# Depthwise convolution of the mixers: two channel blocks on TensorE from four-tap stacks in four column tiles, one block on VectorE

## The reference, cut to what matters

```python
def conv_module(val, gate, w_dw, b_dw, ln_g, ln_b, w_pw, b_pw):
    h = val * jax.nn.sigmoid(gate)                       # (1, 256, 384)
    h = lax.conv_general_dilated(                        # causal, 31 taps, one filter per channel
        h, w_dw[:, None, :], window_strides=(1,),
        padding=((CONV_WIDTH_2 - 1, 0),),
        dimension_numbers=('NWC', 'WIO', 'NWC'),
        feature_group_count=D_CONV) + b_dw
    h = jax.nn.silu(layer_norm(h, ln_g, ln_b))
    return h @ w_pw + b_pw
```

## Time and profile before

| | |
|---|---|
| median of three runs | 1805.52 us (1805.26 to 1806.93) |
| the profiled execution: its own time | 1807.05 us |
| its span, first to last instruction | 1805.3 us |
| granted TensorE clock, mean | 0.996 |
| TensorE busy | 1738.2 us (96%) |
| VectorE busy | 1184.4 us (66%) |
| ScalarE busy | 915.0 us (51%) |
| GpSimd busy | 55.9 us (3%), 54.4 of it the diagonals |
| the 62 records a layer of L1027 (31 products, two passes each) | 13.42 us in layer 1 |

### The profile page before, as it was taken

How to read it: one execution, slowest core, us unless ns; L and a number is a source line. 1 busy time by engine, 2 the same in 40 slices (tenths; PEclk the granted TensorE clock), 3 DMA queues, 4 the chain that set the end, 5 groups by cost and what they waited for, 6 DMA issues and landing times.

```text
span 1805.3 us, 25215 instructions
## 1 busy us (share of the span) xinstructions
PE 1738.2 (96%) x10391; PEld 1425.7 (79%) x10391; DVE 1184.4 (66%) x1517; ACT 915.0 (51%) x992; POOL 55.9 (3%) x71
## 2 busy tenths in 40 slices
PE   7999998999999999999999999999999999999997
PEld 7988897899998999998777777776776777676774
DVE  6664576766798665579677665665665665765653
ACT  5445655555564444345565553554455554554542
POOL 0000000000060000050000000000000000000000
PEclk9999999999999999999999999999999999999999
DMA  9423443565544365645669999999999999999996
GB/s 325 153 94 124 150 146 102 178 233 196 164 157 142 133 220 184 203 126 208 233 210 344 374 398 385 398 396 396 398 391 378 396 396 398 398 398 398 397 397 252
DMA packets 243562, 495.14 MB, mean 274 GB/s; under 512 B 9609, under 2 KB 99439, under 8 KB 229103
## 3 DMA queue, kind: packets, MB, share of 16 engines
q1 hardware_dynamic: 238927, 489.04, 74.0%
q10 hardware_dynamic: 4512, 4.40, 0.9%
HBM read 492.36 MB, written 1.05 MB: 273 GB/s over the span
## 4 chain that ended last, share of the span: by engine, by line
PE 81%; DVE 10%; ACT 6%; issue 2%; DMA 0%; ACTq 0%; DVEq 0%
PE bank L567 22%; PE bank L569 21%; PE bank L568 21%; DVE splitL L2159 6%; PE bank L1233 4%; PE bank L1266 4%; ACT splitH L1461 4%; PE bank L1212 1%; DVE co L2615 1%; PE bank L1168 1%; PE bank L1027 1%; PE bank L596 1%; PE bank L710 1%; PE bank L733 0%; PE bank L1085 0%
## 5 line engine op out<-in xcount | busy, mean ns | idle before, releaser
L2159 DVE TENSOR_TENSOR splitL<-raw,splitH 128x2048 fp32r<-128x2048 f32 (+1 forms) x248 | 561.8, 2273 | 155.3 <-ACT splitH L1461 154.5
L1461 ACT ACTIVATE splitH<-raw 128x2048 fp32r<-128x2048 f32 (+2 forms) x250 | 469.5, 1889 | 123.2 <-PE bank L569 102.4
L567 PE MATMUL bank<-RAH,splitH 128*128 128x256 f32 x1088 | 312.5, 287 | 6.0 <-DVE RAL L2169 3.3
L568 PE MATMUL bank<-RAL,splitH 128*128 128x256 f32 x1088 | 308.5, 284 | 0.0
L569 PE MATMUL bank<-RAH,splitL 128*128 128x256 f32 x1088 | 308.5, 284 | 0.0
L567 PE MATMUL bank<-splitH,RBH 128*128 128x512 f32 x736 | 293.5, 399 | 3.3 <-DVE splitL L2159 3.3
L569 PE MATMUL bank<-splitH,RBL 128*128 128x512 f32 x736 | 287.4, 391 | 0.0
L568 PE MATMUL bank<-splitL,RBH 128*128 128x512 f32 x736 | 286.9, 390 | 0.0
L2159 DVE TENSOR_TENSOR splitL<-rawx,splitH 128x2048 fp32r<-128x2048 f32 x89 | 203.2, 2290 | 28.7 <-ACT splitH L1461 28.2
L567 PEld LDWEIGHTS bank<-RAH,splitH 128*128 128x128 f32 x1088 | 209.3, 192 | 10.4 <-DVE RAL L2169 4.5
L568 PEld LDWEIGHTS bank<-RAL,splitH 128*128 128x128 f32 x1088 | 209.4, 192 | 1.0
(11 more groups left out here) (340 smaller groups left out, 2223.6 us busy)
## 6 DMA issues: line engine op xcount, KB each, us to landing
raw<-in_moe_wg SPq DMA_DIRECT2D x71, 1024.0 KB, 10.4
raw<-in_moe_wd SPq DMA_DIRECT2D x69, 1024.0 KB, 11.5
raw<-in_moe_wu SPq DMA_DIRECT2D x68, 1024.0 KB, 11.2
rawx<-in_moe_wu SPq DMA_DIRECT2D x44, 1024.0 KB, 11.6
rawx<-in_moe_wd SPq DMA_DIRECT2D x43, 1024.0 KB, 12.4
rawx<-in_moe_wg SPq DMA_DIRECT2D x41, 1024.0 KB, 11.8
raw<-in_w_in SPq DMA_DIRECT2D x24, 1024.0 KB, 6.2
raw<-in_w_up SPq DMA_DIRECT2D x22, 1024.0 KB, 5.1
```

What stands on the lines that cost most here:

```text
L567: e.matmul(o, lh, rh, start=start, stop=False)
L568: e.matmul(o, lh, rl, start=False, stop=False)
L1461: return e.activation(o, src, ACT.Copy)
L2159: e.tensor_tensor(l[:, 0:size], raws[home[n]][:, 0:size], h[:, 0:size].bitcast(F), ALU.subtract)\
```

## The change

TensorE takes two blocks, 2 and 0 (in that order, v = 0 and 1), and VectorE keeps block 1. A product now sums over 4 taps x 32 channels on its 128 partitions and yields 32 channels. Four such products with i = 0 to 3 go to partitions 32i to 32i+31 of one bank, each in its own column tile; 8 groups g of four taps make the (padded) 32 taps, so a block has 8 x 4 = 32 products of 32 weight columns and 256 moving columns, and a layer has 64.

The moving data `hs[v]` hold for each i four copies of 32 channels of `hc`, copy j shifted by j columns. ScalarE makes them by DMA from SBUF to SBUF, 16 DMAs a block, 32 a layer. The weights `stack` come ready from DRAM, one DMA of 1 MB a layer, issued by ScalarE. GpSimd's diagonals go.

```diff
@@ tensor, mixers(l) @@
-                b = bank["dw", l] = ring.take()
-                t.wait_ge(S.dwdiag, 32 * l + 31)
-                t.wait_ge(S.th, 3 * l + 3)
-                o = claim(b, (S.co0, l + 1))
-                for k in range(31):
-                    mm = e.matmul(o[:, 0:256], diag[:, k, :], hc[:, 0, 2 + k:258 + k], start=(k == 0), stop=(k == 30))
-                mm.then_inc(S.dw, 1)
+                t.wait_ge(S.in_layer, 96 * (l + 1))
+                for v in range(2):
+                    b = bank["dw", l, v] = ring.take()
+                    t.wait_ge(S.hs, 512 * l + 256 * v + 256)
+                    o = claim(b, (S.co0, 2 * l + v + 1))
+                    for g in range(8):
+                        for i in range(4):
+                            mm = e.matmul(o[32 * i:32 * i + 32, 0:256], stack[:, v, i, g, :],
+                                          hs[v][:, i, 2 + 4 * g:258 + 4 * g], start=(g == 0), stop=(g == 7))
+                    mm.then_inc(S.dw, 1)
@@ scalar, mixers(l) @@
+                def shifted(v, u):
+                    a.wait_ge(S.th, 3 * l + v + 2)
+                    a.wait_ge(S.zero, 4)
+                    if v:
+                        a.wait_ge(S.hs, 512 * l + 256)
+                    for i in range(4):
+                        for j in range(4):
+                            load(hs[v][32 * j:32 * j + 32, i, :], hc[32 * i:32 * i + 32, u, j:j + 288], S.hs)
+
+                load(stack[:, :, :, :, :].rearrange("p v i g c -> p (v i g c)"), stacks[l], S.in_layer)
                 hi_to(mc[0] + 1)
 ...
                 take(mc[2])
+                shifted(0, 2)
                 gate_of(2, 0)
                 for _ in v_rows(mv, 384, lambda tb: vn[:, tb, :], S.mrow, slot, root):
                     pass
+                shifted(1, 0)
                 a.wait_ge(S.mrow, 6 * l + 2)
 ...
-                a.wait_ge(S.dw, l + 1)
-                e.activation(co[:, 0, :], banks[bank["dw", l]][:, 0:256], ACT.Identity,
-                             bias=pcol("conv_dw_b_2", 3 * l)).then_inc(S.co0, 1)
+                for v in range(2):
+                    a.wait_ge(S.dw, 2 * l + v + 1)
+                    e.activation(co[:, 2 - 2 * v, :], banks[bank["dw", l, v]][:, 0:256], ACT.Identity,
+                                 bias=pcol("conv_dw_b_2", 3 * l + 2 - 2 * v)).then_inc(S.co0, 1)
@@ vector, mixers(l): taps() now runs over k = 0 to 30 of block 1 alone @@
@@ gpsimd @@
+            e.memset(hc[:, :, 288:292], 0.0).then_inc(S.zero, 1)
             for l in range(2):
-                dwc = PCOL["conv_dw_w_2"] + 93 * l
-                g.wait_ge(S.xadd, 12 + 8 * l)
-                for k in range(31):
-                    e.tensor_scalar(diag[:, k, :], ident, prm[:, dwc + 3 * k:dwc + 3 * k + 1], None, ALU.mult)\
-                        .then_inc(S.dwdiag, 1)
```

More of the change, by code:

```diff
@@ L149, in halves, with program @@
     return (0, 2, 1, 3).index(tb_half) + 1
-def program(nc, x, mem, consts, w, out, cap):
+def program(nc, x, mem, consts, stacks, w, out, cap):
     ctx = ExitStack()
@@ L175, in program @@
         BL = [at(f"BL{i}", [128, 768], b0 + 64 * KB + 3 * KB * i) for i in range(2)]
-        diag = at("diag", [128, 31, 128], b0 + 64 * KB)
+        stack = at("stack", [128, 2, 4, 8, 32], b0 + 64 * KB)
+        hs = [at("hs2", [128, 4, 288], b0 + 72 * KB)]
         b0 += 40 * KB
@@ L1056, in mixers @@
                         b = bank["colsum", l] = ring.take()
-                        t.wait_ge(S.taps, 62 * (l + 1))
-                        t.wait_ge(S.co0, l + 1)
+                        t.wait_ge(S.taps, 31 * (l + 1))
+                        t.wait_ge(S.co0, 2 * l + 2)
                         o = claim(b, (S.dd, 6 * l + 3))
@@ L2598, in mixers @@
                 dwc = PCOL["conv_dw_w_2"] + 93 * l
-                tapped = [62 * l]
+                tapped = [31 * l]
                 def taps():
-                    at = {}
-                    order = [(k, 1) for k in range(3)]
-                    order += [(k - 3 * (u == 2), u) for k in range(3, 34) for u in (1, 2)]
-                    for k, u in order:
-                        if k < 31:
-                            o, src = co[:, u, :], hc[:, u, 2 + k:258 + k]
-                            wk = prm[:, dwc + u + 3 * k:dwc + u + 3 * k + 1]
-                            if k == 0:
-                                v.wait_ge(S.th, 3 * l + u)
-                                ins = e.tensor_scalar(o, src, wk, pcol("conv_dw_b_2", 3 * l + u), ALU.mult, ALU.add)
-                            else:
-                                v.wait_ge(S.taps, at[u])
-                                ins = e.scalar_tensor_tensor(o, src, wk, o, ALU.mult, ALU.add)
-                            ins.then_inc(S.taps, 1)
-                            tapped[0] += 1
-                            at[u] = tapped[0]
-                            yield
+                    o = co[:, 1, :]
+                    for k in range(31):
+                        src = hc[:, 1, 2 + k:258 + k]
+                        wk = prm[:, dwc + 1 + 3 * k:dwc + 1 + 3 * k + 1]
+                        if k == 0:
+                            v.wait_ge(S.th, 3 * l + 1)
+                            ins = e.tensor_scalar(o, src, wk, pcol("conv_dw_b_2", 3 * l + 1), ALU.mult, ALU.add)
+                        else:
+                            v.wait_ge(S.taps, tapped[0])
+                            ins = e.scalar_tensor_tensor(o, src, wk, o, ALU.mult, ALU.add)
+                        ins.then_inc(S.taps, 1)
+                        tapped[0] += 1
+                        yield
                 more = taps()
@@ L3245, with tap_stacks @@
            "ffn_wu_2", "ffn_wd_2", "moe_router_2", "moe_wg_2", "moe_wu_2", "moe_wd_2", "final_g_2"]
+def tap_stacks(taps):
+    rows = np.zeros((2, 32, 384), np.float32)
+    rows[:, 0:31] = taps
+    rows = rows.reshape(2, 8, 4, 3, 4, 32).transpose(0, 2, 5, 3, 4, 1)[:, :, :, [2, 0]]
+    stacks = np.zeros((2, 4, 32, 2, 4, 8, 32), np.float32)
+    for c in range(32):
+        stacks[:, :, c, :, :, :, c] = rows[:, :, c]
+    return stacks.reshape(2, 128, 2048)
 def kernel(**inputs):
@@ L3259 @@
     out = nc.dram_tensor("out_0", (1, 256, 1024), F, kind="ExternalOutput").ap()
-    program(nc, aps["x"], aps["mem"], aps["shape_constants"], {n: aps[n] for n in WEIGHTS}, out, CAP)
+    program(nc, aps["x"], aps["mem"], aps["shape_constants"], aps["stacks"], {n: aps[n] for n in WEIGHTS}, out, CAP)
     r = run_bass_kernel_spmd(nc, [feeds], core_ids=[0])
```

32 lines of the change are left out of this document (17 added, 15 removed).

## The result

The changed kernel takes 1816.49 us (median of five runs, 1812.85 to 1818.42), beside 1806.93 us for the kernel before in five runs (1805.26 to 1807.50). The ratio is 1.0054, with a 95% interval of 1.0043 to 1.0066. The forecast was 1799.2 us with a range to 1804.5. Among the rivals it is the slow DMA issues, which had 8% and gave 1811 us.

The account below looks back on a forecast made before the run. TensorE was taken to bound the kernel (81% of the chain); gains of 3.8 us in layer 0 and 3.9 in layer 1, less 1.4 for the clock, make 6.3 us: 1799.2 us from the median 1805.52, range 1793.5 to 1804.5.

Parts of the forecast that it names:

- the slow DMA issues: Rival, 8%: each issue holds ScalarE; slower than before from 0.51 us an issue, 1811 us at 0.6 us.
- TensorE's saving: Convolution on TensorE: four column tiles side by side take 7.1 instead of 13.5 us, 6.4 us saved in each layer.
- VectorE's saving: 31 taps fewer on VectorE, 12.3 us a layer, of which 0.48 us count in layer 0 and none in layer 1.
- ScalarE's issues: 16 DMAs issued in one go, twice a layer, on ScalarE: 0.37 us each, 5.9 us a group.
- The first group "fits": 16 issues ahead of the third sigmoid: 5.9 us fit in ScalarE's idle 6.52 and 6.51 us, costing nothing.
- The second group: 16 issues behind `vn`: `at_rows` late by 2.8 and 2.5 us in layers 0 and 1, lost by TensorE in full.
- The data of `hs`: Both groups issued by about 540 us, convolution begins at about 551, so a latency of several us is hidden.
- The clock: Longer TensorE waits ahead of the pooling may lower its granted clock: 1.4 us lost for both layers together.
- The stack's issue: Ahead of the second group of `RAH` on ScalarE: 0.3 us lost in layer 0, nothing in layer 1.
- The experts: TensorE sets the pace there, so time saved ahead stays saved; rival that they swallow it, 6%, 1805.5 us.
- tiles one after another: Rival, 4%: column tiles don't run side by side, the convolution takes 27.6 us a layer; 1837 us.
- the cheap issues: Rival, 4%: ScalarE's issues take 0.2 us or less, nothing is late; 13.3 us gained, 1792.3 us.

Follow-up runs that it names:

- the filled wait: The changed kernel with 15 products of constants (6.5 us) added on TensorE ahead of its wait for `at_rows`; 1813.85 us, ratio 1.0035.

## Why the prediction was wrong, step by step

- **TensorE's saving: right.** 7.1 us forecast, 7.05 measured in both layers, 6.46 us saved. The four tiles run at 0.98 of the ideal (32 x 0.216 = 6.9); the row of two tiles had given 0.96. The 8.7 us, estimated from the Trainium skill (TensorE: Matmul & The Clock Gate, "Part 3: Packing small matmuls"), didn't come.
- **VectorE's saving: right.** 0.48 us in layer 0, none in layer 1. But 31 x 0.397 was too much for what it is relieved of: see the last section.
- **ScalarE's issues: the step that failed.** "At 0.37 a group takes 5.9 us." An issue took 0.641 us and a group 10.3. I had sized it by ten small loads from DRAM on SyncE, and these DMAs have their source in SBUF. No row of the trace before showed such an issue; it was a case for a bound from further off. That trace had longer ones on ScalarE itself, from DRAM: the shortest for `pool_w` (32 KB) took 0.61 us, and the rows of 1.5 us were set aside as queued behind others. My own rival put the point of change of sign at 0.51 us. The range should have gone beyond 1811.
- **The first group "fits", cost nothing: wrong by the same number.** The third sigmoid comes 2.1 us late (531.31 against 529.25), with it the splits behind it and TensorE, which waits 2.77 us at 535.91. The rival's own rule, 16 s - 6.5, gives 3.8 us at 0.641; it is less because the first issue, at 520.37 us, goes out while ScalarE is still at the splits ahead of the group.
- **The second group: the rule holds in number, in part by luck.** The squares are 12.3 us late (546.16 us, against the end of `vn` at 533.82 in the earlier trace rows), less 3.1 us of idle time: 9.2, and the pooling was 8.93 late. With the measured 10.3 it is 10.3 - 3.1 + 2.1 = 9.3, and 10.3 - 3.4 + 2.1 = 9.0 in layer 1. That `at_rows` is late by a group less the idle time is right. That the group begins where `vn` ends was taken for granted, and two things that the sum left out cancel there: the sequencer would have run about 3 us ahead, and the wait for the first group's landing held it back by as much.
- **The data of `hs`, "Even a latency of several us is hidden": wrong for ScalarE.** It held for TensorE, which loses no time on `hs`. But the second group waits for the first to land, in ScalarE's stream, and this was put at nothing: 3.3 and 2.7 us by the estimate above.
- **The clock: undersized.** 1.4 us for both layers; 2.29 and 1.91 were measured. The waits were 7.3 and 8.4 us and not 3.4. The nearest to 3.4 is 4.27 us, in layer 0 of the run with only the second group on ScalarE, and 1.7 us were lost behind it. The mechanism is shown by the filled wait.
- **The stack's issue: 0.3 us forecast, nothing found.** TensorE reaches the first slab `mv` 0.4 us earlier than before (520.48 against 520.89 us).
- **The experts: right.** What is lost ahead of them is lost at the end.

With 10.3 us a group, the sigmoid's measured 2.1 us (together 9.1 us a layer) and the measured clock, the sum of the prediction is 2 x (6.4 - 9.1) + 0.5 - 4.2 = -9.1 us, and 9.6 us slower was measured. With 0.641 in its own rules alone, 3.8 us for the first group in place of 2.1, it would be about 12.6 us slower. Two of its sums are a little off by their own terms, without weight for the forecast: tiles one after another give 1838 and not 1837, and the cheap issues 1792.2.

## What to carry to other kernels

A DMA issued by an engine that computes is an instruction of that engine. Count the issues, take the length of one from a transfer with the same kind of source, and ask what the engine was to do next. Then look for waits for a landing in the same stream: here the second group waited for the first, and that took away the time in which its issues could have run beside the engine's own work. If no row shows such a transfer, the sign of the change may hang on it; then make few large DMAs of many small ones (an overlapping access pattern made 4 of 16 here), or give them to an engine that idles. Either turned a loss of 0.5% into a gain of 0.6 to 0.7%.

Moving a stalling block of work within one stream can merely move the stall: here, behind `at_rows`, it cost as much as ahead of it.

## What the runs showed of the hardware

- An issue from SBUF held its engine 0.64 us on ScalarE and 0.63 on SyncE, whatever was moved from 4 KB to 144 KB. From DRAM, in the same shape, it was 0.47 and 0.45. On GpSimd the instruction that issues from SBUF shows 0.50 us.
- DMA issues run ahead beside the engine's own computing: of 10.4 us of issues 7.26 showed as idle time. A wait for a landing ahead of them stops this: the issues then came 0.07 to 0.08 us behind the landing.
- Four column tiles of 32 columns run as one where they alternate in the stream; where eight products of one tile follow each other they take 0.215 us a record, except around a change of tile.
- VectorE's taps went from 0.397 to 0.521 us each. Before, taps of two blocks alternated; now each waits, by a semaphore, for the one just before it. The run with block 2's taps left out of the kernel before shows the same 0.521 us. Whether the semaphore or the data set it is not shown. The timeline of VectorE, a portion of 5 taps in the kernel before and in the changed one:

```profile
533.72 2.06 DVE L2615 SCALAR_TENSOR_TENSOR co<-hc,prm,co 128x256 f32<-128x256 f32 x5
```

```profile
535.78 2.56 DVE L2631 SCALAR_TENSOR_TENSOR co<-hc,prm,co 128x256 f32<-128x256 f32 x5
```

- A wait of TensorE of 2.8 us was followed by the lower clock in one kernel (0.59 over 4 us) and by the full clock in another, at the same place. What decides it there is open.
